# ScalarE copies the next head's queries in slots 3 and 5 of a step, and the ring has six row buffers in place of eight

## What is computed

```
for each token x (after RMSNorm), for each of 8 heads:
    q = x @ wq[head]                      # two halves of 128
    s = q_half @ subkeys[head, half].T    # 128 scores for each half
    top 16 of each half, top 16 of their 256 sums -> 16 expert numbers e, 16 gates (softmax)
    act_k = gelu(u_tab[e_k] . x)          # one row of 1024 floats for each expert
    y    += gate_k * act_k * v_tab[e_k]   # another row of 1024 floats
h = h + y ;  out = RMSNorm(h)
```

## Time and profile before

| | |
|---|---|
| median of 3 runs | 3162.5 us (3161.84 to 3164.97) |
| the profiled execution | 3164.81 us, of which span 3163.0 us |
| DVE, PE, ACT, POOL busy | 65%, 74%, 43%, 36% of the span |
| expert phase: first gather issued, last dot begins | 576.8 us, 3149.7 us |
| mean granted TensorE clock | 0.83 of 2.4 GHz |

### The profile page before, as it was taken

How to read it: one execution, slowest core, us unless ns; L and a number is a source line. 1 busy time by engine, 2 the same in 40 slices (tenths; PEclk the granted TensorE clock), 3 DMA queues, 4 the chain that set the end, 5 groups by cost and what they waited for, 6 DMA issues and landing times.

```text
span 3163.0 us, 36373 instructions
## 1 busy us (share of the span) xinstructions
PE 2352.9 (74%) x11880; PEld 897.3 (28%) x11880; DVE 2047.2 (65%) x4903; ACT 1364.5 (43%) x4011; POOL 1134.8 (36%) x1073
## 2 busy tenths in 40 slices
PE   8998987677677776777777767776777777777766
PEld 4655554322222222222222222222222222222211
DVE  1566673566666666666666666666666666666664
ACT  3143444344444444444444444444444444444443
POOL 1000000344444444443444434443444444444442
PEclk9999987788888878888888778877888888877776
DMA  3300000999999999999999999999999999999997
GB/s 110 120 27 27 20 7 25 390 426 427 427 426 423 426 426 413 427 425 426 419 418 424 426 424 421 424 427 425 410 425 426 426 414 423 426 424 426 420 426 332
DMA packets 184964, 1121.65 MB, mean 355 GB/s; under 512 B 19520, under 2 KB 45248, under 8 KB 53584
## 3 DMA queue, kind: packets, MB, share of 16 engines
q0 software_dynamic: 147456, 1073.81, 80.9%
q1 hardware_dynamic: 37328, 45.63, 4.3%
HBM read 1110.97 MB, written 8.39 MB: 354 GB/s over the span
## 4 chain that ended last, share of the span: by engine, by line
DMA 55%; PE 14%; ACT 5%; DVE 4%; issue 3%; POOL 2%; SPq 0%; DVEq 0%; ACTq 0%; POOLq 0%
DMA ring<-table,e_odd 28%; DMA ring<-table,e_even 26%; PE acc_odd L1350 5%; PE acc_even L1350 4%; DVE ring L1248 4%; PE qq_ps L1326 3%; PE proj L1307 2%; POOL ring L993 2%; ACT diag L1083 1%; ACT weight L1076 1%; ACT gelu L1100 1%; DMA wq_rest<-wq 1%; ACT L1100 1%; ACT L1058 0%; PE s_ps L1341 0%
## 5 line engine op out<-in xcount | busy, mean ns | idle before, releaser
L1248 DVE CUSTOM_DVE_ANT_0 ring<-ring,xn_odd 128x1024 f32<-128x1024 f32 x512 | 627.2, 1225 | 423.9 <-DMA ring<-table,e_odd 219.8
L1248 DVE CUSTOM_DVE_ANT_0 ring<-ring,xn_even 128x1024 f32<-128x1024 f32 x512 | 627.1, 1225 | 406.7 <-DMA ring<-table,e_odd 210.0
L1350 PE MATMUL acc_odd<-ring,diag 64*64 64x512 f32 x4096 | 674.5, 755 | 231.9 <-ACT diag L1083 231.1
L993 POOL DMA_INDIRECT ring<-table,e_even x512 | 549.6, 1074 | 767.8 <-PE acc_odd L1350 356.7
L1350 PE MATMUL acc_even<-ring,diag 64*64 64x512 f32 x4096 | 651.2, 732 | 216.1 <-ACT diag L1083 215.4
L993 POOL DMA_INDIRECT ring<-table,e_odd x512 | 552.5, 1079 | 712.7 <-PE acc_odd L1350 334.6
L1100 ACT ACTIVATE gelu<-dots 128x1 f32<-128x1 f32 x1024 | 207.5, 203 | 1349.5 <-DVE dots L1248 1345.9
L1083 ACT ACTIVATE diag<-pairs,weight 128x64 f32<-128x64 f32 x1024 | 356.0, 348 | 33.5
L1350 PEld LDWEIGHTS acc_odd<-ring,diag 64*64 64x64 f32 x4096 | 134.2, 156 | 635.2 <-ACT diag L1083 533.1
L1350 PEld LDWEIGHTS acc_even<-ring,diag 64*64 64x64 f32 x4096 | 132.6, 152 | 587.4 <-ACT diag L1083 473.7
L1326 PE MATMUL qq_ps<-wq_rest,xnT_cur 128*128 128x256 f32 x896 | 266.4, 436 | 8.4 <-DMA wq_rest<-wq 8.4
(11 more groups left out here) (191 smaller groups left out, 2112.1 us busy)
## 6 DMA issues: line engine op xcount, KB each, us to landing
w_slot<-w_in SPq DMA_DIRECT2D x16, 512.0 KB, 4.0
ring<-table,e_even POOLq DMA_INDIRECT x512, 15.5
ring<-table,e_odd POOLq DMA_INDIRECT x512, 15.1
wq_rest<-wq SPq DMA_DIRECT2D x1, 7168.0 KB, 23.4
w_out_s<-x SPq DMA_DIRECT2D x8, 512.0 KB, 3.9
w_out_s<-w_out SPq DMA_DIRECT2D x1, 4096.0 KB, 12.8
h_next<-x SPq DMA_DIRECT2D x8, 512.0 KB, 8.1
mix_t<-mix_dram SPq DMA_DIRECT2D x7, 512.0 KB, 7.8
```

The source lines that it names most:

```text
L993: pool.indirect_dma_start(out=ring[:, g % RING, :], out_offset=None, in_=table[:, :], in_offset=bass.IndirectOffsetOnAxis(ap=e_row[m % 2][ ...
L1248: dve.tensor_tensor_reduce(ring[:, g % RING, 0:D], ring[:, g % RING, 0:D], xn[(m // PH) % 2][:], 1.0, 0.0, ALU.mult, ALU.add, dots[:, k:k ...
L1350: ins = pe.matmul(acc[t % 2][ROWS[j], HALF[i]], diag[ROWS[i], g % DIAGS, :], ring[ROWS[i], g % RING, D + j * 512:D + (j + 1) * 512], start ...
```

## The change

The ring has six buffers in place of eight. ACT copies the queries out in slot 3 (was 6) and the transposed ones in slot 5 (was 8). PE takes the key scores after combine k = 8 in place of 6 in the first head of tiles 1 to 7; there they also wait for DVE's read of the two columns in `s_ps` (`b_lvar`). Nothing else differs.

```diff
-RING = 8
+RING = 6
...
                     if k == 4 and m + 1 < NSTEPS:
                         gate_exp(m + 1)
-                    if k == 6 and m + 2 < NSTEPS:
+                    if k == 3 and m + 2 < NSTEPS:
                         queries(m + 2)
-                    if k == 8 and m + 2 < NSTEPS:
+                    if k == 5 and m + 2 < NSTEPS:
                         queries_t(m + 2)
...
                 if r >= 1:
                     pe.wait_ge(b_r, ROUTE_STEPS * (r - 1) + 3)
+                if r > PH and r % PH == 2:
+                    pe.wait_ge(b_lvar, r // PH)
...
-                        elif k == 6:
+                        elif k == (8 if t >= 1 and h == 0 else 6):
                             key_scores(m + 2)
```

## The result

The changed kernel is slower: 3176.8 us (3174.6 to 3182.3, 5 runs) against 3163.3 us (3161.8 to 3165.0, 5 runs) for the kernel before, a ratio of 1.0048 [1.0037, 1.0059]. That is 13.6 us, above the 0.2% that a measurement can tell. The same file run again against other runs of before gave 3177.2 us, 1.0041 [1.0027, 1.0056]. The profiled execution took 3182.3 us, span 3180.4; it is the slowest of its five, 17.5 us above that of before, and what follows is read from it.

The account below looks back on a forecast made before the run. The expert phase was taken as a DMA-bound stream of 1024 gathers, 2.45 us each. Plain steps 0, tile starts 3 and phase start 2 us gave +5 on 3162.5: 3167.5 us, range 3160 to 3180.

Parts of the forecast that it names:

- (c): First step of tiles 1 to 7: gather 12 goes out 1.2 to 4.5 us late; 0.4 us a tile, 3 us taken.
- the slower rival: Reserve too small in plain steps: ACT's slot 3 copy comes 2 to 5 us late behind PE's projection; +16, 3178; chance 0.16.
- 0.4 us of waiting: ACT's query copy in slot 3 waits this long for the projection in the step shown, at no cost.
- (a): ACT's exponentials stay in slot 4, so the gelu after the next dot begins 1.5 us late.
- (b): Heads 0 to 3: the next tile's projection behind combine 5 makes combine 6 late by 0.5 to 3 us.
- Together 4.55. The reserve is ... 6.5 us: Ring of six: 11.05 us allowed from issue to landing, 4.55 needed by a gather without queue, leaving 6.5 us for delays.
- 0 us for about 55 steps: Plain steps lose nothing, because their delays of 2 to 4.5 us stay inside a reserve of 5.6 to 6.5.
- (d): Start of the expert phase: eighth gather's dot at 602.3, 0.6 us late, plus 1.4 for the first step; together 2 us.
- (e): Key scores after combine 8 in seven steps: no new wait, 0 us.
- (f): Gain: today's idle DMA, some 0.6 us at each tile, could go; taken as 0, at most 4 us.
- The lead covers everything: Rival: one DMA engine is always the slow one, its queue never empty; +0 to +2, 3163.5 us; chance 0.20.
- The clock rule: PE's clock halves after idling, so the removed wait lifts it in slots 5 and 6; sum +2, 3164.5; not adopted.

## Why the prediction was right or wrong

The forecast was 3167.5 us and "the same", the measured median 3176.8: inside the range, on the slower side, 9 us beyond the forecast: +13.6 us where +5 was forecast. That it stayed under the upper end, 3180, is in part luck. That end was set by (c) without a lead and by the slower rival, and neither is what happened in heads 1 to 3.

- **What bounds it: right.** The phase stayed a stream of gathers at DMA's pace, and the landings in the chain went from 15 to about 11 us.
- **The moved copies: right.** Worth nothing alone (0.9998), and needed for six buffers (+90 us without them). "0.4 us of waiting" on ACT was the right kind: 55.7 us in 39 steps, for free.
- **(a) and (b), "together 2 to 4.5 us": right in size.** In the step shown it was 1.5 us for the gelu and 4.45 us in all.
- **The step that failed: "Together 4.55. The reserve is ... 6.5 us", and from it "0 us for about 55 steps".** The sum counts up to the landing, and a gather lands when the slowest of the 16 engines has done its share. The others run out of work sooner: in the step above ten of them had finished gather 11 at 1057.1 to 1057.5, some 2.5 us before its dot (1059.83). For them gather 12 was due that much earlier, and of 6.5 us some 4 are left (an estimate, 6.5 - 2.5). Gather 12 was 4.45 us late: it found them empty, and with the long packets behind the hole its dot came 1.1 us late. The prediction knew of the others' lead over the slowest engine, but used it only to make (c) cheaper. In heads 1 to 3 of tiles 1 to 6 it came to 11.6 us, 5.8 when what heads 4 to 7 gave back is taken off, where 0 was forecast (7.4 and 2.9 in the second profile). The same too large reserve stands behind the terms (c) and (d).
- **What the three cures show.** Either delay moved, or the table loads removed, takes away 9.7 us or more of the loss, so their meeting is its cause. How they meet is not taken apart: in each of the three the projection also ran faster (665, 703 and 727 ns a matmul, against 962 and 911 in the two profiles of the changed kernel), because PE had idled less ahead of it or because it stood elsewhere. In the step shown the low clock makes 1.6 us of the projection and 0.9 of combine 5, out of 4.45 in all.
- **(c), "gather 12 goes out between 1247.9 and 1251.2": right; its price, "0.4 a tile", wasn't.** Tile 2's first step, timeline, after:

```profile
1245.97 1.23 DVE L1248 CUSTOM_DVE_ANT_0 ring<-ring,xn_even 128x1024 f32<-128x1024 f32 x1 [0.78 <-DMA ring<-table,e_even]
...
1252.78 3.31 PE L1307 MATMUL proj<-w_out_s,mix_t 128*128 128x512 f32 x4
...
1257.41 0.94 POOL L993 DMA_INDIRECT ring<-table,e_even  x1 [3.33 <-PE acc_even L1352]
...
1273.45 1.22 DVE L1248 CUSTOM_DVE_ANT_0 ring<-ring,xn_even 128x1024 f32<-128x1024 f32 x1 [2.54 <-DMA ring<-table,e_even]
```

 Dot 5 begins at 1245.97, 7.22 later than before, so the issue at 1257.41 stands at 1250.2 of before. Dot 15, at 1273.45, waited 2.54 us. From dot 5 to dot 2 of the next step it took 35.6 us (to 1281.59), where before took 33.5 (1238.75 to 1272.28). The lead of the faster DMA engines did not cover it. It is no fixed 4 to 5 us either. Ahead of this gather 12 the others fell idle at 1258.1, 2.5 us before the dot of gather 11 (1260.58). Before, they fell idle ahead of gather 14, at 1252.8, and that was 6.0 us before the dot of gather 13 (1258.84). So 2.1 us were lost here, 1.5 a tile on average, 8.9 in six tiles. Before's own 33.5 us are 1.7 more than 13 periods of 2.45. The other transfers in that stretch, 0.52 MB, took 1.4 us of the 16 engines, so "delayed no dot I could find" holds to some 0.3 us. The count of "seven tiles" was one too many: tile 7 has no projection behind combine 5, and its first step lost nothing.
- **(d), the start: right in the gather, too small in the sum.** The eighth gather's dot begins at 600.62 in an execution whose first gather went out 1.83 us earlier, so at 602.45 against the 602.3 worked out. But the first dots and tile 0 lost 5.1 us together (8.2 in the second profile), and 2 were taken. The first seven gathers and what followed, after:

```profile
574.99 1.13 POOL L993 DMA_INDIRECT ring<-table,e_even  x1 [23.90 <-DVE e_even L1234]
...
591.64 0.94 POOL L993 DMA_INDIRECT ring<-table,e_even  x1 [9.31 <-PE acc_even L1352]
...
600.62 1.23 DVE L1248 CUSTOM_DVE_ANT_0 ring<-ring,xn_even 128x1024 f32<-128x1024 f32 x1 [0.79 <-DMA ring<-table,e_even]
...
605.90 0.94 POOL L993 DMA_INDIRECT ring<-table,e_even  x1 [3.25 <-PE acc_even L1352]
```

- **(e) and (f): right.** No wait for the key scores appears, and no version came out faster by more than its interval.
- **The slower rival, "+16, 3178": the right size by another mechanism.** It asked for copies 2 to 5 us late behind the projection. That wait never exceeded 2.8 us, and it stands in two kernels that lose nothing. Its "32 steps with a projection" are 28, since the last tile has none.
- **The lead covers everything: refuted for the changed kernel.** A lead did not hide the late issues of a tile's first step. Which engine is the slow one, no row tells. "The rate is the same with the queue long or short", under *Faster*, held with eight buffers only: 423 GB/s over the phase became 420 with six and 397 with five.
- **The clock rule.** The wait that left PE was replaced by another in the next slot, for the diagonal (2.48 us in the step shown), so PE idled on, and the projection behind it ran at 1.2 GHz more often than before, mean 962 ns a matmul against 844 (after, then before):

```profile
L1307 PE MATMUL proj<-w_out_s,mix_t 128*128 128x512 f32 x224 | 182.6, 962 | 0.0
L1307 PE MATMUL proj<-w_out_s,mix_t 128*128 128x512 f32 x224 | 158.2, 844 | 0.0
```

 The sum by the rule, +2, was not borne out. The Trainium skill (TensorE: Matmul & The Clock Gate, Part 1: The HAM clock gate) has the clock halved after idling. The step shown agrees: after 2.48 us of idling the projection took 3.57 us, and 1.99 in slot 9, where the combine ahead of it had waited 1.39. The clock alone does not decide either: with eight buffers and 891 ns nothing is lost.

**What stays open.** How the delays and the clock share the loss, as said. How much of a late dot is the hole and how much the long packets behind it, since the trace doesn't say which engine a packet is on. About 4 us remain with either delay moved, 3.2 us with seven buffers. In the trace with the projection in slot 9, 3.5 of 4.5 us lie in the first dots and tile 0; part of that may be the start itself, whose first 8 dots take 0.7 us more even with eight buffers, and no run separated it. With the exponentials in slot 7, 2.0 us lie in head 4 of the tiles, which no run explains. By what heads 4 to 7 win back 5.8 us was not tried. No version beats the kernel before: the one with eight buffers and moved copies equals it.

## What to carry to other kernels

Count the reserve of a ring up to the moment at which the first DMA engines run out of work, not up to the landing, which the slowest engine makes: here that took some 2.5 us off a reserve of 6.5, and with five buffers the whole stream starved. Look for lost throughput in windows of half a microsecond behind a late issue. A share over several microseconds stayed near 1 here, because the long packets behind a hole make up for the hole. Before a ring is cut, list the delays that fall on the same buffer and move one of them away; either one of two took away some 10 of 13.6 us here, and a wait that costs nothing today may be what only the deep queue hides.

## What the runs showed that was not expected

- **Most DMA engines run empty for a moment, and their packets are long after it.** Counted from the packets between 640 and 3100 us: spells in which fewer than 14 of the 16 engines had a packet on its way came 30 times and made 18.8 us in the changed kernel, 11 times and 7.5 us before. Of the 30, 18 lie at gather 12 of a step with a projection. With the projection in slot 9 they made 5.1 us, without table loads 3.3, with five buffers 95.5. Packets of gathers over 320 ns number 1082 before and 2295 after. Over the same stretch, what packets took beyond 309 ns is 12.8 us an engine more than before, and 10.3 of these stand within 5 us of the start of such a spell. So the slowing mostly follows an empty spell. Why the packets grow was not tried.
- **The rate of the phase.** Over the phase the stream held 423 GB/s with eight gathers in flight, 420 with six and 397 with five, and 426 in whole stretches, with one core at work. The Trainium skill (DMA: Bandwidth & Descriptors, Measured) has 425 GB/s for a transfer of 16 MB and 341 for one of 1 MB. The stream agrees with the first, though each gather is 1 MB; no run here had a single one in flight.
